# A hybrid decoder step in fp32: four dense projections by Strassen's scheme

## The chip, the core and the metric

The kernel runs on one core of a Trainium2 chip. The core has five engines that run their own instruction streams and meet at semaphores: TensorE (PE, matmuls from SBUF into PSUM), VectorE (DVE), ScalarE (ACT), GpSimd (POOL) and SyncE (SP, which issues the DMAs here). The metric is the device time of one execution in microseconds (us); smaller is better. All arithmetic here is fp32.

## The reference, cut to what matters

One layer step for 512 prompt tokens and 8 sample tokens, 520 in all: a sparse attention branch and a state-space branch, both from one normalised input, are mixed through gates and go through a gated feed-forward part. Only the end of it is changed:

```python
def merge_and_ffn(x, attn_o, ssm_o, ga, gm, w_attn_br, w_ssm_br, w_out, norm2_w, w_ffn_gate, w_ffn_up, w_ffn_down):
    mix = sigmoid(ga) * (attn_o @ w_attn_br) + sigmoid(gm) * (ssm_o @ w_ssm_br)
    x = x + mix @ w_out                                   # 1024 -> 1024, the out-projection
    h = rmsnorm(x, norm2_w)
    return x + (silu(h @ w_ffn_gate) * (h @ w_ffn_up)) @ w_ffn_down   # 1024 -> 2816 twice, 2816 -> 1024
# both outputs then go through rmsnorm(., normf_w)
```

## The kernel before, in words

**Layout.** Activations lie with features on the 128 partitions and the 520 tokens along the free axis: `xT` (the residual stream, 8 tiles of 128 features), `xn` (normalised, 8 tiles), `mix` (8 tiles), `hid` (22 tiles of the feed-forward's inner width), `stage` and `gate` (2 tiles each). Weights are streamed through `ring`, six slots of 1 MB, each holding 1024 rows (8 blocks of 128) by 256 columns of a weight matrix.

**A dense tile.** `dense` (the matmul is L351) makes one output tile of 128 features: for each of the row blocks k, two matmuls with the same 128x128 block of weights, one for each half of the tokens (TH = 260 columns), into a pair of PSUM banks. Two pairs of banks are used in turn. A tile of the out-projection, gate or up is 8 x 2 matmuls, one of down 22 x 2. So the part in question is 8 tiles of out-projection, 44 of gate and up, 8 of down.

**Around it.** ScalarE reads each finished tile out of PSUM (L1398 for out-projection and down, L1412, L1413 and L1417 in the feed-forward part), which frees the bank pair (`dense_read`). In `residual` VectorE adds the copy to `xT` (L1800), ScalarE squares the new tile (L421) and VectorE adds the squares up (L427); when all eight are in, TensorE sums over partitions (L379), ScalarE takes the root, VectorE the reciprocal, TensorE spreads it (L387, L388), ScalarE copies it (L405, L406), and VectorE writes the eight tiles of `xn` (L434). This happens after the out-projection (norm 2) and after down (final norm). In `ffn` ScalarE forms tanh of a half of the gate tile and a halved copy of it in `hid`, and VectorE multiplies (L1814) and then multiplies in the up tile (L1818).

**Order.** Each engine's order is its program text. TensorE: the attention part of the mix (4 steps of two gate tiles and two branch tiles), the out-projection, norm 2, gate and up in 11 steps of two gate and two up tiles, down, the final norm, the turning back of the output. SyncE loads the next block of weights into a slot as soon as `dense_done` says that the slot's tiles are done; four slots (5, 0, 1, 2) take gate and up in turn, 3 and 4 are filled early for down. GpSimd has nothing to do after the gathers of the decode part: its last work is L1929.

Of the kernel before, what the change touches and what calls it, by code (L numbers as in the profile page):

```python
# [76 lines left out]
def build(nc, x_prompt, x_sample, cache_k, cache_v, cache_idx_k, state_ssm, state_conv, page_table,  # L77
# [5 lines left out]
    with ExitStack() as ctx:  # L83
# [19 lines left out]
        gs = sb("gs", [32, GSEL])  # L103
# [188 lines left out]
        ytok, ystok = xtok, xstok  # L292
        raw_flat = raw.rearrange("p i t -> p (i t)")
# [10 lines left out]
        DOWN_SLOTS = [(3, 4, 1), (2, 5, 0)]  # L304
# [13 lines left out]
        F_DOWN = [21, 12, 16, 6, 6, 11]  # L318
# [10 lines left out]
        w_in_slot = [S(f"weights_in_slot{i}") for i in range(NSLOT)]  # L329
# [80 lines left out]
        def rms_pe(pe, i, e):  # L410
            pe.wait_ge(S("squares_added"), 7 * i + 5)
            sum_squares(pe, e, sqsum)
            spread_norm(pe, e)

        def square(act, i, k, ready=None):

            if ready is not None:
                act.wait_ge(S("res_added"), ready + k + 1)
            if k >= 3:
                act.wait_ge(S("squares_added"), 7 * i + k - 4)  # L420
            act.activation(sqsum if k == 0 else sq2[:, k % 2, :], xT[:, k, :], ACT.Square).then_inc(S("norm_squared"), 1)  # L421

        def add_square(v, i, k):
# [3 lines left out]
            v.tensor_tensor(sqsum, sqsum, sq2[:, k % 2, :], ALU.add).then_inc(S("squares_added"), 1)  # L427

        def rms_dve(v, i, e, w_col):
# [3 lines left out]
            for k in range(KT):  # L433
                v.scalar_tensor_tensor(xn[:, k, :], xT[:, k, :], vec[:, w_col + k:w_col + k + 1], rbc,  # L434
# [6 lines left out]
        def _(sp):  # L441
# [34 lines left out]
            sp.wait_ge(S("iqs_copied"), 1)  # L476
# [60 lines left out]
            def load_selectors(g):  # L537
                sp.dma_start(gs[:], gsel_d[bass.ds(g, 1)].rearrange("o p c -> (o p) c")
# [65 lines left out]
            for it in range(2):  # L604
                n = N_ATT + 14 if it == 0 else N_OUT + 2
                load(sp, FFN_SLOTS[it][0], w_block(w_ffn_gate, it * 256), n)
                load(sp, FFN_SLOTS[it][1], w_block(w_ffn_up, it * 256), n + 2)
            load(sp, 3, w_block(w_ffn_down, 0), N_OUT + 6)
            load(sp, 4, w_block(w_ffn_down, 0, k0=D), N_OUT + 8)
            with sp.Fori(0, 4) as k:  # L610
                for o in range(2):
                    load(sp, FFN_SLOTS[o][0], w_block(w_ffn_gate, 512 * k + 256 * (o + 2)), 8 * k + N_FFN + 4 * o + 2)
                    load(sp, FFN_SLOTS[o][1], w_block(w_ffn_up, 512 * k + 256 * (o + 2)), 8 * k + N_FFN + 4 * o + 4)
            load(sp, FFN_SLOTS[0][0], w_block(w_ffn_gate, 2560), N_FFN + 34)
            load(sp, FFN_SLOTS[0][1], w_block(w_ffn_up, 2560), N_FFN + 36)
            for it in range(4):
                for i, slot in enumerate(DOWN_SLOTS[it % 2]):
                    if it == 0 and i < 2:
                        continue
                    freed = N_DOWN + 2 * (it - 1) if it > 1 else {1: N_FFN + 38, 2: N_FFN + 40, 5: N_FFN + 42, 0: N_FFN + 44}[slot]  # L620
                    load(sp, slot, w_block(w_ffn_down, 256 * it, k0=D * i, kt=(8, 8, 6)[i]), freed)
# [14 lines left out]
        def _(pe):  # L636
# [103 lines left out]
            pe.wait_ge(S("ik_sq"), 1)  # L740
# [331 lines left out]
            def ffn(k, o):  # L1072
                for s in range(2):
                    slot = FFN_SLOTS[o][s]
                    pe.wait_ge(w_in_slot[slot], 16 * (k + F_FFN[slot] + 1))
                    for j in range(2):
                        first = isinstance(k, int) and k + o + s + j == 0
                        dense(pe, 8 * k + N_FFN + 4 * o + 2 * s + j, j, block_of(slot, j), xns,
                              ready=("norm_ready", KT) if first else None)

            ffn(0, 0)
            ffn(0, 1)
            with pe.Fori(1, 5) as k:
                ffn(k, 0)
                ffn(k, 1)
            ffn(5, 0)

            def down(it, k):

                slots = DOWN_SLOTS[it]  # L1090
                for s in slots:
                    pe.wait_ge(w_in_slot[s], 16 * (k + F_DOWN[s] + 1))
                for j in range(2):
                    blocks = block_of(slots[0], j) + block_of(slots[1], j) + block_of(slots[2], j, 6)
                    dense(pe, 4 * k + N_DOWN + 2 * it + j, j, blocks, [hid[:, i, :] for i in range(FT)],
                          ready=("hid_ready", 2 * OPEN) if isinstance(k, int) and k + it + j == 0 else None)

            down(0, 0)
            down(1, 0)
            down(0, 1)  # L1100
            down(1, 1)
            rms_pe(pe, 2, NORMF)

            pe.wait_ge(S("dense_read"), N_END)
# [13 lines left out]
        def _(act):  # L1118
# [21 lines left out]
            act.activation(taps, ps[:, 4, 128:256], ACT.Copy, scale=0.5).then_inc(S("taps_ready"), 1)  # L1140
            act.activation(dsk, ps[:, 4, 256:272], ACT.Copy).then_inc(S("dsk_ready"), 1)
# [7 lines left out]
            act.activation(hvec[0:32, 2:3], hvec[0:32, 1:2], ACT.Exp).then_inc(S("a_exp"), 1)  # L1149
            act.wait_ge(S("vector_mark"), IK_SQ_IN)  # L1150
            act.activation(ikt2, ikt1, ACT.Square).then_inc(S("ik_sq"), 1)
# [5 lines left out]
            act.activation(iqs, kviq[:, 4:12, SEQ:T], ACT.Copy).then_inc(S("iqs_copied"), 1)  # L1157
            act.wait_ge(S("tensor_mark"), IK_VAR)
            act.activation(two(ikt2), ps[:, 4:6, 0:TH], ACT.Sqrt, bias=eps[:, 0:1]).then_inc(S("ik_root"), 1)
# [5 lines left out]
            act.activation(actok, ps[:, 7, 256:384].rearrange("p (b h) -> p b h", h=32), ACT.Copy).then_inc(S("actok_ready"), 1)  # L1165
# [29 lines left out]
            act.activation(qkvs[:, 0:8, :], uT[:, :, SEQ:T], ACT.Copy).then_inc(S("qkvs_ready"), 1)  # L1195
            act.activation(qkvs[:, 8:12, :], kviq[:, 0:4, SEQ:T], ACT.Copy).then_inc(S("qkvs_ready"), 1)
# [192 lines left out]
            def residual(n0, before, i):  # L1389
                for n in range(8):  # L1390
                    act.wait_ge(S("dense_done"), n0 + n + 1)
                    if n >= 2:
                        act.wait_ge(S("res_added"), before + n - 1)
                    else:
                        act.wait_ge(S("mixed"), 16)
                        if before:
# [594 lines left out]
```

## Time and profile before

| | us |
|---|---|
| median of 3 runs | 1762.99 |
| lowest and highest | 1761.59, 1771.35 |
| the profiled execution's span (the page gives no other time of it) | 1790.0 |
| TensorE busy in the span | 1685.6 |
| VectorE, ScalarE, GpSimd busy | 764.1, 400.6, 217.7 |

A page is one execution, seen by the hardware profiler. "Busy" is the time in which an engine executes; "idle before" is the time in which it stood still just before an instruction, with what released it; the chain follows the last instruction back through whatever it waited for. One fp32 matmul leaves two records.

### The profile page before, as it was taken

To read this page: it belongs to the slowest core of one execution; us is meant where nothing else is said; L and a number is where in the kernel's file an instruction comes from. 1 tells how busy PE (TensorE), PEld (TensorE's weight loads), DVE (VectorE), ACT (ScalarE), POOL (GpSimd) and SP (SyncE) were. 2 spreads that over 40 slices of the span, in tenths; PEclk is the share of its full clock that TensorE was granted. 3 is DMA by queue.
4 is the path that set the end of the run, shared out by engine and by line. 5 is a ranking of instruction groups with operands and counts; after the bars stand their busy time and mean duration, and the time that the engine had idled before them with its cause. 6 is when DMAs were issued, how large, how long until landed. Compare 5 with 4: busy or idle time off the path is not lost. (4 is left out here: it accounts for less than half of the span.)

```text
span 1790.0 us, 21883 instructions
## 1 busy us (share of the span) xinstructions
PE 1685.6 (94%) x8411; PEld 1430.7 (80%) x8411; DVE 764.1 (43%) x1192; ACT 400.6 (22%) x855; POOL 217.7 (12%) x224
## 2 busy tenths in 40 slices
PE   6998998999999999999889799999999999999997
PEld 5886876887777778878768688888788888888886
DVE  3314886179989999898871000001120101000002
ACT  3013236224334342243320010000211111110002
POOL 1000110024122231241221500000000000000000
PEclk8998989999999999999999879899999999999997
DMA  6111122223313313221224404122212222221201
GB/s 196 47 36 48 47 66 79 72 68 83 95 54 97 97 54 96 56 72 47 78 71 139 123 1 141 48 71 83 82 48 71 83 81 70 70 65 56 92 0 48
DMA packets 153482, 131.12 MB, mean 73 GB/s; under 512 B 11410, under 2 KB 149938, under 8 KB 153410
## 3 DMA queue, kind: packets, MB, share of 16 engines
q1 hardware_dynamic: 150610, 121.93, 22.6%
q0 software_dynamic: 2816, 8.39, 1.6%
q8 instruction: 42, 0.69, 0.2%
q14 instruction: 14, 0.11, 0.0%
HBM read 117.26 MB, written 13.27 MB: 73 GB/s over the span
## 5 line engine op out<-in xcount | busy, mean ns | idle before, releaser
L351 PE MATMUL ps<-xn,ring 128*128 128x260 f32 x4160 | 945.4, 387 | 7.6 <-DVE xn L434 3.3
L351 PEld LDWEIGHTS ps<-xn,ring 128*128 128x128 f32 x4160 | 789.4, 191 | 134.2 <-issue 3.8
L351 PE MATMUL ps<-work,ring 128*128 128x260 f32 x960 | 210.7, 382 | 0.0
L351 PEld LDWEIGHTS ps<-work,ring 128*128 128x128 f32 x960 | 182.4, 190 | 28.0
L351 PE MATMUL ps<-ssm_o,ring 128*128 128x260 f32 x512 | 120.9, 399 | 2.8 <-issue 2.8
L351 PEld LDWEIGHTS ps<-ssm_o,ring 128*128 128x128 f32 x512 | 102.2, 200 | 20.4 <-issue 3.4
L1800 DVE TENSOR_TENSOR xT<-xT,work 128x520 f32<-128x520 f32 x16 | 11.2, 700 | 192.3 <-ACT work L1398 192.3
L1907 POOL TENSOR_TENSOR ring<-ring 128x512 f32<-128x512 f32 x32 | 40.5, 1265 | 331.8 <-ACT ring L1261 331.8
L1814 DVE SCALAR_TENSOR_TENSOR work<-work 128x520 f32 (+1 forms) x22 | 15.4, 700 | 145.9 <-ACT work L1413 145.9
L1596 DVE MAX8 work<-work 8x8 f32<-8x2049 f32 x32 | 72.8, 2273 | 0.6
L1601 DVE FIND_INDEX8 dix<-work 8x8 uint32<-8x2049 f32 x32 | 72.8, 2274 | 0.0
L1603 DVE MATCH_REPLACE8 work<-work 8x2049 f32<-8x2049 f32 x32 | 72.5, 2266 | 0.0
L1818 DVE TENSOR_TENSOR work<-work 128x520 f32 (+1 forms) x22 | 15.4, 700 | 130.8 <-ACT work L1417 130.8
L1635 DVE SCALAR_TENSOR_TENSOR work<-work 128x512 f32<-128x512 f32 x96 | 67.0, 769 | 7.3 <-ACT work L1271 7.3
L1734 DVE SCALAR_TENSOR_TENSOR work<-work 128x520 f32<-128x520 f32 x8 | 5.6, 700 | 136.7 <-ACT work L1351 114.5
L351 PE MATMUL ps<-uT,ring 128*128 128x260 f32 x256 | 59.6, 395 | 0.4 <-DVE uT L1784 0.4
L351 PEld LDWEIGHTS ps<-uT,ring 128*128 128x128 f32 x256 | 50.4, 198 | 8.7 <-DVE uT L1784 0.5
L1257 ACT ACTIVATE ring<-ps,work 128x128 f32<-128x128 f32 x128 | 36.5, 367 | 79.3 <-PE ps L910 79.3
L1398 ACT ACTIVATE work<-ps 128x520 f32<-128x520 f32 x16 | 9.7, 603 | 194.4 <-PE ps L351 194.4
L1231 ACT ACTIVATE work<-ps 128x520 f32<-128x520 f32 x32 | 18.2, 593 | 129.1 <-PE ps L351 129.1
L1790 DVE SCALAR_TENSOR_TENSOR work<-work 128x520 f32<-128x520 f32 x8 | 5.6, 700 | 91.8 <-ACT work L1387 91.8
L1417 ACT ACTIVATE work<-ps 128x520 f32<-128x520 f32 x22 | 13.3, 604 | 134.8 <-PE ps L351 134.8
(299 smaller groups left out, 1711.6 us busy)
## 6 DMA issues: line engine op xcount, KB each, us to landing
ring<-in_w_in SPq DMA_DIRECT2D x34, 1024.0 KB, 5.3
ring<-in_w_ffn_gate SPq DMA_DIRECT2D x11, 1024.0 KB, 5.3
ring<-in_w_ffn_up SPq DMA_DIRECT2D x11, 1024.0 KB, 5.3
ring<-in_w_in SPq DMA_DIRECT2D x16, 512.0 KB, 5.3
work<-in_state_ssm SPq DMA_DIRECT2D x16, 512.0 KB, 6.3
out<-work SPq DMA_DIRECT2D x16, 512.0 KB, 4.0
ring<-in_w_ssm_br SPq DMA_DIRECT2D x8, 1024.0 KB, 6.5
ring<-in_w_ffn_down SPq DMA_DIRECT2D x8, 1024.0 KB, 5.1
```

The lines of the kernel that those rows point to most:

```text
L351: mm = pe.matmul(ps[0:m, 2 * pair + h, 0:TH], lhs[k], rhs[k][:, h * TH:(h + 1) * TH], start=(k == 0), stop=(k == len(lhs) - 1))
L1231: act.activation(two(raw[:, i, 3:T + 3]), tile_out(i % 2), ACT.Copy).then_inc(S("dense_read"), 1)
L1257: act.activation(M2[:, c % 2, r * P:(r + 1) * P], abc[:, r * P:(r + 1) * P], ACT.Relu, scale=-1.0, bias=atg[:, c, r:r + 1]).then_inc(S("E_ ...
L1417: act.activation(two(stage[:, j, :]), tile_out(j), ACT.Copy).then_inc(S("dense_read"), 1)
L1596: v.max(best, row).then_inc(S("dtop_max"), 1)
L1601: v.max_index(dix[:], best, row).then_inc(S("dtop_index"), 1)
L1603: v.match_replace(row, best, row, -3.3e38).then_inc(S("dtop_cut"), 1)
L1635: v.scalar_tensor_tensor(xc[:, i, 0:SEQ], raw[:, i, t:t + SEQ], cw[:, 5 * i + t:5 * i + t + 1], xc[:, i, 0:SEQ], ALU.mult, ALU.add).then_i ...
L1800: v.tensor_tensor(xT[:, n, :], xT[:, n, :], stage[:, n % 2, :], ALU.add).then_inc(S("res_added"), 1)
L1814: v.scalar_tensor_tensor(hs[j], gate[:, j, :], 1.0, hs[j], ALU.add, ALU.mult).then_inc(S("silu_h"), 1)
L1818: v.tensor_tensor(hs[j], hs[j], stage[:, j, :], ALU.mult).then_inc(S("hid_ready"), 1)
L1907: g.tensor_tensor(m, m, CBm[:, c:c + 1, :].broadcast_to((P, 4, P)), ALU.mult).then_inc(S("M_ready"), 1)
```

## The change

Every pair of output tiles (256 columns of weights) of the out-projection, gate, up and down becomes one *unit*, numbered q: 0 to 3 out-projection, 4 to 25 gate and up in turn, 26 to 29 down. In a unit the weights are seen as 2 x 2 blocks, a11, a12, a21, a22 (first index the tile, second the parity of the row block), and the activations as b11, b12, b21, b22 (parity of the row block, half of the tokens). In place of eight block products there are seven, each a chain of 4 matmuls of 260 columns (11 in down):

- GpSimd makes, for each unit, s1 = a21 + a22, s3 = a11 - a21 (in place of a21), s2 = s1 - a11 and s4 = a12 - s2, each for all row pairs at once (128 x 512 elements, for down three pieces of 512, 512 and 384). It may start when the third product of the unit two before is done, since two sets of sum buffers are used in turn.
- VectorE makes, once for `mix`, `xn` and `hid`, the four sums of each pair of tiles: t1 = b12 - b11, t3 = b22 - b12, t2 = b22 - t1, t4 = b21 - t2 (260 columns each, t2 after t1, t4 after t2).
- TensorE's order within a unit is product 6 (s2 t2), 7 (s3 t3), 2 (a12 b21, added onto product 1 in its bank), 5 (s1 t1, onto product 6), then product 1 (a11 b11) of the next unit, then 3 (s4 b22, onto 6 and 5) and 4 (a22 t4, onto 7). Three banks are used by a unit, two sets in turn.
- ScalarE copies product 1 (`copy_1`) and the finished first quarter (`copy_11`); VectorE forms the other three quarters in five additions of 260 columns from PSUM (`add_u2`, `add_others`). What follows (residual, squares, tanh, multiplies) works on both tiles of a unit after that, instead of tile by tile.

The last three groups of down's weights go to space of `xn` and `uT` in turn with the ring; a slot is refilled after the last product of its unit (`load_after`) where it was after the tile before. Some semaphores of the first part are merged (`ik_sq`, `iqs_copied` and `ik_root` into `ik_steps`, `a_exp` into `dt_exp`, `taps_ready` and `dsk_ready` into `vec_ready`, `gone_ready` into `dpg_ready`), and `gs` gets 128 rows instead of 32, the rest used for sums.

The core of the diff:

```diff
+        def operands(q):
+            a = [[], [], [], [], [], [], []]
+            for (slot, n, _), (s1, s2, s4) in zip(units(q), pair_sums(q)):
+                parts = (quarter(slot, n, 0, 0), quarter(slot, n, 0, 1), s4, quarter(slot, n, 1, 1), s1, s2, quarter(slot, n, 1, 0))
+                for of, part in zip(a, parts):
+                    of += [part[:, k, :] for k in range(n)]
+            b, t = (MIX_B, MIX_T) if q < Q_FFN else (XN_B, XN_T) if q < Q_DOWN else (HID_B, HID_T)
+            return a, [b[0][0], b[1][0], b[1][1], t[3], t[0], t[1], t[2]]
...
+        def load_after(sp, q, slot, src):
+            sp.wait_ge(S("product_done"), 6 * q + DONE_4)
+            kt, n = src.shape[1], src.shape[2]
+            sp.dma_start(slots[slot][:, 0:kt, 0:n], src).then_inc(w_in_slot[slot], 16)
...
         @block.tensor
-            for u in range(4):
-                pe.wait_ge(w_in_slot[OUT_SLOTS[u]], 16 * (F_OUT[OUT_SLOTS[u]] + 1))
-                for j in range(2):
-                    dense(pe, N_OUT + 2 * u + j, j, block_of(OUT_SLOTS[u], j), [mix[:, k, :] for k in range(KT)],
-                          ready=("mixed", 8) if u + j == 0 else None)
+            def product_6(q, m0=0, m1=None, sums=None):
+                if m0 == 0:
+                    pe.wait_ge(S("weight_sums"), 4 * unit_number(q + 1) - 1)
+                    if q >= 2:
+                        pe.wait_ge(S("combined"), 5 * (q - 2) + MADE_C12)
+                mm = product(q, 1, 5, m0, m1, sums=None if sums is None else sums + 3)
+                if m1 is None:
+                    mm.then_inc(S("product_done"), 1)
+            def head(q, sums=None):
+                if q >= 2:
+                    pe.wait_ge(S("combined"), 5 * (q - 2) + MADE_C21)
+                product(q, 2, 6, sums=None if sums is None else sums + 2).then_inc(S("product_done"), 1)
+                pe.wait_ge(S("s1_copied"), q + 1)
+                product(q, 0, 1, start=False, stop=True).then_inc(S("product_done"), 1)
+                pe.wait_ge(S("combined"), 5 * q + MADE_U2)
+                product(q, 1, 4, start=False).then_inc(S("product_done"), 1)
+            def tail(q, sums=None):
+                pe.wait_ge(S("weight_sums"), 4 * unit_number(q + 1))
+                pe.wait_ge(S("combined"), 5 * q + MADE_U4)
+                product(q, 1, 2, start=False, stop=True).then_inc(S("product_done"), 1)
+                pe.wait_ge(S("combined"), 5 * q + MADE_C22)
+                product(q, 2, 3, start=False, stop=True, sums=None if sums is None else sums + 4).then_inc(S("product_done"), 1)
+            pe.wait_ge(S("dense_read"), N_OUT)
+            product_1(0, ready=("mixed", 8))
+            for q in range(Q_OUT, Q_FFN):
+                first = SUMS_MIX if q == Q_OUT else None
+                product_6(q, sums=first)
+                head(q, sums=first)
+                if q + 1 < Q_FFN:
+                    product_1(q + 1)
+                tail(q, sums=first)
             rms_pe(pe, 1, NORM2)
+            product_1(Q_FFN, ready=("norm_ready", KT))
...
         @block.scalar
+            def residual(q0, before, i):
+                for u in range(4):
...
+                        act.wait_ge(S("res_added"), before + 2 * u)
+                    copy_1(q0 + u, stages)
+                    if u:
+                        square(act, i, 2 * u - 2, before)
+                        square(act, i, 2 * u - 1, before)
+                    copy_11(q0 + u, stages)
...
         @block.vector
+            def sums(b, t, m, base):
+                v.tensor_tensor(t[0][m], b[0][1][m], b[0][0][m], ALU.subtract).then_inc(S("sums_made"), 1)
+                v.tensor_tensor(t[2][m], b[1][1][m], b[0][1][m], ALU.subtract).then_inc(S("sums_made"), 1)
+                v.wait_ge(S("sums_made"), base + 4 * m + 2)
+                v.tensor_tensor(t[1][m], b[1][1][m], t[0][m], ALU.subtract).then_inc(S("sums_made"), 1)
+                v.wait_ge(S("sums_made"), base + 4 * m + 3)
+                v.tensor_tensor(t[3][m], b[1][0][m], t[1][m], ALU.subtract).then_inc(S("sums_made"), 1)
...
             rms_dve(v, 1, NORM2, 8)
+            for m in range(4):
+                v.wait_ge(S("norm_ready"), KT + 2 * m + 2)
+                sums(XN_B, XN_T, m, SUMS_XN)
...
         @block.gpsimd
+            g.wait_ge(S("vector_mark"), DO_READY)
+            for q in range(Q_OUT, Q_END):
+                if q >= 2:
+                    g.wait_ge(S("product_done"), 6 * (q - 2) + DONE_3)
+                for i, ((slot, n, filled), (s1, s2, s4)) in enumerate(zip(units(q), pair_sums(q))):
...
+                    g.wait_ge(w_in_slot[slot], filled)
+                    g.tensor_tensor(s1, a21, a22, ALU.add).then_inc(S("weight_sums"), 1)
+                    g.wait_ge(S("weight_sums"), done + 1)
+                    g.tensor_tensor(a21, a11, a21, ALU.subtract).then_inc(S("weight_sums"), 1)
+                    g.tensor_tensor(s2, s1, a11, ALU.subtract).then_inc(S("weight_sums"), 1)
+                    g.wait_ge(S("weight_sums"), done + 3)
+                    g.tensor_tensor(s4, a12, s2, ALU.subtract).then_inc(S("weight_sums"), 1)
```

## Rows read from the trace of the kernel before

**Rows 1.** The page: engine totals, and the chain's shares by line.
```profile
PE 1685.6 (94%) x8411; PEld 1430.7 (80%) x8411; DVE 764.1 (43%) x1192; ACT 400.6 (22%) x855; POOL 217.7 (12%) x224
...
PE ps L351 42%; PE ps L1024 1%; PE ps L1056 1%; PE ps L387 0%; PE ps L1012 0%; PE ps L1112 0%; DVE xn L434 0%; PE ps L379 0%; PE ps L388 0%; ACT ssm_o L1431 0%; DVE ssm_o L427 0%; DVE xT L1800 0%; ACT ssm_o L421 0%; ACT work L1398 0%; ACT rt L395 0%
```

**Rows 2.** The chain from 1130 us: start, us, what, records.
```profile
1134.61 157.27 PE ps L351 x704
...
1291.91 0.61 ACT work L1398
...
1294.72 1.19 PE ps L379 x10
...
1300.44 464.86 PE ps L351 x2112
```

**Rows 3.** Timeline of TensorE: start, us, instruction, records, idle before.
```profile
1134.61 16.99 PE L351 MATMUL ps<-uT,ring 128*128 128x260 f32 x64 [0.43 <-DVE uT L1784]
1151.44 14.19 PE L351 MATMUL ps<-xn,ring 128*128 128x260 f32 x64
1165.47 14.19 PE L351 MATMUL ps<-uT,ring 128*128 128x260 f32 x64
...
1235.60 56.27 PE L351 MATMUL ps<-work,ring 128*128 128x260 f32 x256
```

**Rows 4.** Groups of instructions: count, busy us, mean ns, idle before.
```profile
L351 PE MATMUL ps<-work,ring 128*128 128x260 f32 x960 | 210.7, 382 | 0.0
```

**Rows 5.** The same view, GpSimd.
```profile
L1907 POOL TENSOR_TENSOR ring<-ring 128x512 f32<-128x512 f32 x32 | 40.5, 1265 | 331.8 <-ACT ring L1261 331.8
...
L1886 POOL TENSOR_TENSOR work<-work 128x32 f32<-128x32 f32 x24 | 13.6, 592 | 82.0 <-ACT work L1278 82.0
```

**Rows 6.** The page's DMA issues: count, KB each, us to landing.
```profile
ring<-in_w_ffn_gate SPq DMA_DIRECT2D x11, 1024.0 KB, 5.3
```

**Rows 7.** Timeline of VectorE, ops of 256 columns and what follows them.
```profile
430.70 0.42 DVE L1699 TENSOR_TENSOR work<-work 128x256 f32<-128x256 f32 x1 [0.71 <-PE ps L929]
431.16 0.42 DVE L1702 TENSOR_TENSOR work<-work,ps 128x256 f32<-128x256 f32 x1
431.50 0.74 DVE L1709 SCALAR_TENSOR_TENSOR work<-work,ps 128x512 f32<-128x512 f32 x1
```

**Rows 8.** Groups of instructions, ScalarE copying 256 columns from PSUM.
```profile
L1176 ACT ACTIVATE ssm_o<-ps 128x256 f32<-128x256 f32 x16 | 6.1, 382 | 12.5 <-DVE ssm_o L1509 11.3 <-PE ps L648 1.2
```

**Rows 9.** DMA issues from 1687 to 1730 us, three loads issued together.
```profile
ring<-in_w_ffn_down SPq DMA_DIRECT2D x1, 768.0 KB, 9.8
```

**Rows 10.** Timeline of GpSimd.
```profile
443.67 4.75 POOL L1901 TENSOR_TENSOR work<-work 128x1024 f32<-128x1024 f32 x2
```

**Rows 11.** Timeline of VectorE at the same time.
```profile
444.19 1.86 DVE L1639 TENSOR_TENSOR work<-work 128x16 f32<-128x16 f32 x1
445.98 3.61 DVE L1642 SCALAR_TENSOR_TENSOR work<-work 128x520 f32<-128x520 f32 x3
449.74 0.70 DVE L1642 SCALAR_TENSOR_TENSOR work<-work 128x520 f32<-128x520 f32 x1 [0.16 <-ACT work L1292]
```

**Rows 12.** Line L1639: ns at least, in the middle and at most.
```profile
L1639 DVE TENSOR_TENSOR work<-work x8: 221/1863/1867, 377.4 to 871.2; 128x16 f32<-128x16 f32 x8
```

**Rows 13.** Timeline of ScalarE at the end of the mix.
```profile
1235.80 0.60 ACT L1387 ACTIVATE work<-ps 128x520 f32<-128x520 f32 x1 [6.41 <-PE ps L351]
```

**Rows 14.** Timeline of VectorE there.
```profile
1237.17 0.70 DVE L1794 TENSOR_TENSOR work<-work 128x520 f32<-128x520 f32 x1
```

**Rows 15.** Timeline of VectorE at norm 2.
```profile
1299.54 5.46 DVE L434 SCALAR_TENSOR_TENSOR xn<-xT,vec,ssm_o 128x520 f32<-128x520 f32 x8 [2.96 <-ACT ssm_o L406]
```

**Rows 16.** Stretches there and behind: us, busy of PE, PEld, DVE, ACT, POOL, granted clock.
```profile
1301.00:1304.00 3.00, 3.00 (x8) 2.36 (x7) 3.00 (x5) 0.00 (x0) 0.00 (x0) 0.51 0.00 0
1304.00:1308.00 4.00, 4.00 (x20) 3.47 (x19) 0.99 (x2) 0.00 (x0) 0.00 (x0) 1.00 0.02 4
...
1320.00:1400.00 80.00, 80.00 (x366) 69.35 (x365) 7.70 (x11) 10.39 (x17) 0.00 (x0) 1.00 0.22 72
```

More of the change, by code:

```diff
@@ L331, in w_block, with banks @@
+        def banks(q):
+            return [3 * (q % 2) + i for i in range(3)]
         def w_block(w, c0, n=2 * P, k0=0, kt=KT):
@@ L1081, in _ @@
[L1081 to L1101, printed above, removed]
+            def product(q, bank, which, m0=0, m1=None, start=True, stop=False, sums=None):
+                a, b = operands(q)
+                lhs, rhs = a[which], b[which]
+                for m in range(m0, len(lhs) if m1 is None else m1):
+                    if sums is not None:
+                        pe.wait_ge(S("sums_made"), sums + 4 * m)
+                    mm = pe.matmul(ps[:, banks(q)[bank], 0:TH], lhs[m], rhs[m], start=start and m == 0,
+                                   stop=stop and m == len(lhs) - 1, skip_group_check=True)
+                return mm
@@ new lines, in _ @@
+            for q in range(Q_OUT, Q_FFN):
[5 more added lines that the diff above has]
+                tail(q, sums=first)
+            rms_pe(pe, 1, NORM2)
+            product_1(Q_FFN, ready=("norm_ready", KT))
+            for q in range(Q_FFN, Q_DOWN):
+                first = SUMS_XN if q == Q_FFN else None
+                product_6(q, sums=first)
+                head(q, sums=first)
+                if q + 1 < Q_DOWN:
+                    product_1(q + 1)
+                else:
+                    product_1(q + 1, m1=10, ready=("hid_ready", 0))
+                tail(q, sums=first)
@@ new lines, in _ @@
+            for q in range(Q_DOWN, Q_END):
+                first = SUMS_HID if q == Q_DOWN else None
+                if q == Q_DOWN:
+                    product_6(q, m1=10, sums=first)
+                    product_1(q, m0=10, ready=("hid_ready", 0))
+                    product_6(q, m0=10, sums=first)
+                else:
+                    product_6(q)
+                head(q, sums=first)
+                if q + 1 < Q_END:
+                    product_1(q + 1)
+                tail(q, sums=first)
@@ L1424, in _ @@
+            residual(Q_DOWN, KT, 2)
             root_norm(act, NORMF, D)
-            copy_norm(act, NORMF, rbc)
+            copy_norm(act, NORMF, rbcs[2])
             for b in range(5):
@@ new lines, in _ @@
+            for i in range(11):
+                q = Q_FFN + 2 * i
+                h = [hid[:, 2 * i, :], hid[:, 2 * i + 1, :]]
+                add_u2(q, h)
+                if i:
+                    hidden(i - 1)
+                add_others(q, h)
+                add_u2(q + 1, stages)
+                for j in range(2):
+                    v.wait_ge(S("gate_read"), 2 * i + j + 1)
+                    v.scalar_tensor_tensor(h[j], gate[:, j, :], 1.0, h[j], ALU.add, ALU.mult).then_inc(S("silu_h"), 1)
+                add_others(q + 1, stages)
@@ L1825, in _ @@
+            hidden(10)
+            residual(Q_DOWN, 2)
             rms_dve(v, 2, NORMF, 16)
```

294 lines of the change are left out of this document (191 added, 103 removed).

## The prediction

> **What bounds the kernel now.** I read the totals first: TensorE is busy for 1685.6 us of a span of 1790.0, and the chain of work that ended last is 42% line L351, the matmul of `dense` [rows 1]. The shares of the span are an average, so next I read that chain over the part that the change touches, from the last part of the mix to the end [rows 2]. It is one unbroken run of L351 from 1134.61 to 1291.88 us (the mix and the out-projection), a norm of 8.6 us in which TensorE has nearly nothing to do, and a second run from 1300.44 to 1765.30 (gate, up and down). Nothing else ends late there: VectorE and ScalarE only follow. The timeline of TensorE then gives the price of a matmul [rows 3]. 64 records start every 14.03 us, two records belong to one fp32 matmul (the out-projection has 8 tiles x 8 blocks x 2 halves = 128 matmuls and 256 records), so one matmul of 260 columns takes 14.03/32 = **0.4384 us**. The idle time of a group of 960 such records is 0.0, across all tile borders with their waits [rows 4]: a wait that is already satisfied shows no cost here.
>
> The sum is made against the profiled execution. Its span is 1790.0 us, 27.0 above the median of 1762.99, and the page gives no other time for it. All that is removed below lies where the granted clock is 1.00, as in the first 80 us of it [rows 16], so I take the microseconds off the median unscaled.
>
> **What it removes.** Out: 128 matmuls become 4 x 28 = 112. Gate and up: 704 become 22 x 28 = 616. Down: 352 become 4 x 77 = 308. That is 148 fewer, 148 x 0.4384 = **-64.9 us**, all on the path. The moving operand stays 260 columns wide and every matmul loaded its own weights before (one weight load per matmul record), so the price of one stays.
>
> **What it adds beside TensorE, in steady state.** Set time 0 where the sixth product of the unit before ends. A unit of 28 matmuls then takes 12.28 us, in blocks of 1.75: product 6, product 7, product 2 (needs ScalarE's copy of product 1), product 5 (needs the first VectorE sum), product 1 of the next unit, product 3, product 4 (each needs a VectorE read of its bank).
> GpSimd: 4 sums of 128x512 at 1.265 us [rows 5] are 5.1 us, and they may start at product 3 of the unit two before, so some 14 us are there for them. A load of 1 MB lands in 5.3 us [rows 6] with three units (37 us) to do it in. Both are hidden.
> VectorE: 256 columns take 0.42 us, from SBUF or with one operand in PSUM [rows 7]; ScalarE takes 0.38 to copy as many out of PSUM [rows 8]. The first sum waits for product 6 (1.75), is done at 2.2 and needed at 5.26. The one for bank 1 is done at 7.5 and needed at 8.77; bank 2 is read at 7.9 and needed at 10.52. In a gate or up unit the two multiplies (0.70 each) and the four sums of a pair of `hid` (1.6) fit between 2.2 and 7.0. So no handover is late, by margins of 1.2 us and more: cost 0. If that cover goes, the nearest row is TensorE's one wait on a short VectorE step, 0.43 us idle [rows 3]; one such in each of 30 units is +13 us. Between 0 and 13 I take 0, since the idle column reads 0.0 [rows 4], and keep 13 for the range.
> In the down units all these margins grow with the 11 pairs. The last of the three loads behind each lands in 9.8 us [rows 9]; their raw blocks are needed 44 matmuls (19.3 us) after the issue, their sums (12 of at most 1.265, 15.2 us) 33.8 us after it: hidden.
>
> **The lock between VectorE and GpSimd.** The rows show one [rows 10 to 12]. While two GpSimd sums ran from 443.67 to 448.42, a VectorE op on 128x16 with both operands in SBUF took 1.86 us (0.22 at its shortest) and the next op of 128x520 ended only with the second sum; right behind them the same op took 0.70. So a VectorE op with two SBUF operands sits out the GpSimd sum in progress, up to 1.27 us here. GpSimd's four sums run from -1.7 to about 3.4 in my unit's time, with VectorE's ops between them. In a gate or up unit this delays the multiplies to about 4.7 and the sums to 6.4, still before 7.0. In the out-projection it meets the residual adds, which free the staging tile for ScalarE's copy of product 1: the copy, ready at 2.3 without the lock, comes at about 3.8, 0.3 after product 2 wants it. Three units: **+0.9 us**.
> The Trainium skill says the same ("SBUF — State Buffer", section "Who interferes with whom"): a VectorE instruction with two SBUF inputs and a GpSimd instruction that reads SBUF exclude one another, and whoever comes second is blocked. The trace agrees, 1.86 us against 0.22; without that rule and row the two lock terms of my sum would be nothing and the forecast about 1707.
>
> **What it adds on the path.**
> Start of the out-projection: before, its first tile only waited for the tile before the last to be read. Now it waits for ScalarE's last copy, 1235.80 + 0.60 [rows 13]. TensorE idles from 1235.6 to about 1236.4: **+0.75**. The last pair sum that product 6 needs is ready at 1237.87 + 0.34 + 0.45 + 0.42 = 1239.1 [rows 7, 14], wanted at 1239.5: no cost.
> Tail before the norm: before, the last matmul was followed by a copy, an add, a square and an add, until 1294.72: 2.83 us [rows 2]. Now both tiles of the pair end together: a sum of 260 columns, two adds, two squares and two adds, pipelined 3.2 us, so +0.4 for each of two norms. At the first norm GpSimd's sums for the first up unit run at the same time (their buffers came free at product 3 of the last out unit). By the lock, the second add ends at 3.4 instead of 1.7 and the last square's add at 6.0 instead of 3.2: +2.8. Together **+3.6** (bounds 0.8 without the lock, 5.9 with four full waits of 1.27).
> First gate unit: this is the largest term. Before, TensorE followed VectorE's eight `xn` tiles one by one, starting 0.9 us after the first. Now product 1 needs every second tile, and product 6 needs sums that VectorE makes only after all eight, 5.46 us from 1299.54 [rows 15]. A pair's four sums depend on each other; by starts of 0.34 (independent) and 0.46, taken as 0.45 (dependent) [rows 7] a pair takes 1.58 us, and the third sum of the fourth pair is there at 1305.0 + 3 x 1.58 + 0.34 + 0.45 + 0.42 = 1310.95. TensorE has done 8 matmuls by 1311.8 (the last at half clock). The other 916 take 401.6. The granted clock was 0.51 from 1301 to 1304 and 1.00 after it [rows 16]: TensorE had run its first 3.5 us behind the pause at the lower of its two levels (1.2 of 2.4 GHz), which costs 1.75. I expect the same behind the new pause. The end is then 1715.1 against 1765.30, a gain of 50.2 where 132 matmuls fewer would give 57.9: **+7.7**. Bounds: 5.9 if the clock has come back by then, 9.5 if it stays low as long again.
> Semaphores merged under one name in the first 1130 us keep their order and their engines: 0, and 1 us either way for what I miss.
>
> **Sum:** -64.9 + 0.9 + 0.75 + 3.6 + 7.7 = -51.95. 1762.99 - 51.95 = **1711.0 us**.
>
> **The rivals.**
> *Handovers are not free.* The unit splits 28 matmuls into seven chains with some ten waits, where a tile had 16 behind one or two. For it: margins of 1.2 us rest on ops that no row shows with these very operands. Against it: 0.0 idle in 960 records [rows 4]. At 0.43 a unit: 1711.0 + 13 = 1724.
> *VectorE late in each unit.* If the lock lets GpSimd's sums through in a row, an op waits for two of them. In the out, gate and up units a delay of 2 x 1.27 against a margin of 1.26 at bank 1 stalls 1.28 us x 22 units or so: 1711 + 28 = 1739. Against it: GpSimd's sums are over by about 4.7 and the bank 1 sum has only one SBUF operand, while the lock's rows are of two.
> *GpSimd becomes the bound, slower than before.* A unit took 32 x 0.4384 = 14.03 us before; GpSimd decides from 14.03/4 = 3.5 us a sum. For it: GpSimd's strided op on 128x32 took 592 ns [rows 5], 18.5 ns a column, and the new sums read blocks out of a wider tile; at half of that rate a sum of 512 takes 4.7 us. A unit would be 18.9 us, 26 units +127, four down units (56.9 against 38.6) +73: about 1960; at 3.75 us a sum it is still 1815. Against it: the runs here are 128 columns long, as in L1907, which took 1265.
> *The saving isn't there* (the count of matmul records does not fall, or each gets dearer): the same, near 1763. Against it: price and count above.
>
> **Chances.** Forecast 0.68, its own range 1703 to 1718 (the bounds of tail, first gate unit and spread of runs). Handovers 0.20, late VectorE 0.06, no saving 0.02, GpSimd 0.04. The runs before spread over 1761.6 to 1771.4, so 0.5% is about what a measurement tells from no change. Faster: 0.68 + 0.20 + 0.06 = 0.94; same 0.02; slower 0.04. The low end is 1703, all lower bounds together; at the high end 1731 takes in the handovers with the upper bound of the lock.
>
> **What would show it.** Right: 2072 records of L351's successors for out, gate, up and down instead of 2368, still 0.219 us apart; some 12 us from the first `xn` tile to the first dense stretch; VectorE's residual adds over 1 us where a GpSimd sum runs; the stretch from there to the last matmul near 403 us. Wrong: idle of TensorE spread over all units with VectorE or ScalarE as releaser (handovers), with GpSimd as releaser (GpSimd bound), or a record that takes longer than before.

## The result and the profile after

The changed kernel takes **1717.44 us** (median of 4 runs, 1712.1 to 1719.38) against 1763.23 before (median of 4 as well): ratio 0.9717 with a 95% interval of 0.9685 to 0.975, faster. The forecast was 1711.0 with a range of 1703 to 1731. A second set of runs, made for the experiments, gave 1719.23 and 0.9726 [0.9698, 0.9753].

The page of after, and the chain from the end of the mix (start, us, what, records), answer to [rows 1, 2]:

```profile
PE 1616.8 (94%) x8115; PEld 1363.1 (80%) x8115; DVE 884.9 (52%) x1418; ACT 385.9 (23%) x851; POOL 420.1 (25%) x376
...
PE ps L1166 22%; PE ps L445 14%; PE ps L1182 4%; PE ps L1149 1%; DVE xT L2000 1%; DVE xn L528 1%; PE ps L1117 0%; PE ps L481 0%; PE ps L1260 0%; PE ps L473 0%; PE ps L1105 0%; DVE ssm_o L521 0%; DVE uT L1953 0%; ACT ssm_o L1592 0%; DVE work L521 0%
```

```profile
1210.26 0.61 ACT work L1535
...
1250.98 2.81 DVE xT L2000 x2
1253.81 0.40 ACT work L1540
...
1258.06 0.44 DVE work L1977
...
1265.56 1.69 DVE ssm_o L521
...
1274.15 5.46 DVE xn L528 x8
...
1285.14 0.44 DVE uT L1953
1285.63 7.04 PE ps L1166 x26
...
1294.43 10.52 PE ps L1166 x48
...
1306.70 10.52 PE ps L1166 x48
```

L1166 and L1182 are the matmul of a product (L1182 is product 1). TensorE has 8115 records where it had 8411: 296 fewer, two for each of 148 matmuls. What was one run of L351 is now cut at a few places: ScalarE's last copy of the mix (L1535), VectorE's residual adds (L2000), which hold back the copy of product 1 (L1540), its first read of a bank in the last unit (L1977), the sums before the norm (L521), `xn` and the pair sums. From 1285.63 on the chain is TensorE alone as far as the end of down's last unit but one, and a unit of gate or up returns every 12.27 us (1294.43, 1306.70).

**Where the time went, by stage.** Each stage is measured on the timeline of one profiled execution, from the end of the mix's last matmul on. "Front edits" is the experiment e_front, which computes as before did and whose profiled run took 1763.59 us, near its median of 1764.57.

| us | before | front edits | after |
|---|---|---|---|
| end of the mix | 1235.6 | 1207.1 | 1210.1 |
| to the last matmul of the out-projection | 56.27 | 56.27 | 52.32 |
| to norm 2's first sum on TensorE | 2.85 | 2.84 | 5.72 |
| to the first tile of `xn` | 4.82 | 5.25 | 6.05 |
| to the last matmul of down | 465.75 | 466.84 | 415.63 |
| final norm and the rest | 24.71 | 23.51 | 24.02 |
| **from the mix to the end** | **554.4** | **554.7** | **503.7** |

The changed part took 50.7 to 51.0 us less, where the forecast said 51.95. The medians differ by 45.8 only: the runs of either kernel fall into two groups (means 1763.1 and 1771.1 before, 1713.7 and 1719.4 after), group against group the gain is 49.4 and 51.7, but the middle run of before lies in the shorter group and that of after in the longer. The difference arises in the first part, where TensorE does the same work in both kernels. After's profiled execution reached the end of the mix at 1210.1 us and a second one at 1213.5, where four variants of it with the same first part (e_defer, e_xn, e_best, e_pool2) reached it at 1205.1 to 1207.7.

The first 1200 us also clear up the profiled execution of before: it reached the end of the mix 28.5 us later than e_front did with the same instructions, which is the excess that the prediction left out by taking its sum off the median.

### The profile page after: what moved, and what is told of

Read it like the earlier page. It is cut to its first block and busy times, and to the rows that moved or that the text cites. A ratio compares the mean times of both kernels' runs of the same rounds, so it can differ in the third digit from the quotient of the medians.

```text
span 1713.8 us, 21557 instructions
## 1 busy us (share of the span) xinstructions
PE 1616.8 (94%) x8115; PEld 1363.1 (80%) x8115; DVE 884.9 (52%) x1418; ACT 385.9 (23%) x851; POOL 420.1 (25%) x376
## 5 line engine op out<-in xcount | busy, mean ns | idle before, releaser
L445 PE MATMUL ps<-xn,ring 128*128 128x260 f32 (+1 forms) x2752 | 639.0, 390 | 6.0 <-ACT work L1303 1.9
L445 PEld LDWEIGHTS ps<-xn,ring 128*128 128x128 f32 (+1 forms) x2752 | 523.7, 193 | 92.4 <-ACT work L1303 2.3
L445 PE MATMUL ps<-ssm_o,ring 128*128 128x260 f32 x512 | 114.6, 386 | 0.0
L445 PEld LDWEIGHTS ps<-ssm_o,ring 128*128 128x128 f32 x512 | 98.2, 192 | 15.3
L2158 POOL TENSOR_TENSOR work<-ring 128x512 f32<-128x512 f32 (+1 forms) x15 | 18.5, 1233 | 276.4 <-PE ps L1166 154.1
L1166 PE MATMUL ps<-uT,ring 128*128 128x260 f32 x352 | 84.9, 384 | 0.0
L1166 PEld LDWEIGHTS ps<-uT,ring 128*128 128x128 f32 x352 | 67.5, 192 | 10.6
L1977 DVE TENSOR_TENSOR work<-ps,work 128x260 f32<-128x260 f32 x30 | 12.9, 429 | 101.8 <-PE ps L1166 101.8
L1981 DVE TENSOR_TENSOR work<-ps,work 128x260 f32<-128x260 f32 x30 | 12.9, 429 | 100.8 <-PE ps L1166 100.8
L445 PE MATMUL ps<-uT,ring 128*128 128x260 f32 x256 | 58.8, 392 | 0.4 <-DVE uT L1944 0.4
L445 PEld LDWEIGHTS ps<-uT,ring 128*128 128x128 f32 x256 | 49.9, 196 | 8.5 <-DVE uT L1944 0.5
L1545 ACT ACTIVATE work<-ps 128x260 f32<-128x260 f32 x30 | 11.6, 387 | 191.4 <-PE ps L1166 191.4
L1540 ACT ACTIVATE work<-ps 128x260 f32<-128x260 f32 x30 | 11.6, 388 | 179.8 <-DVE xT L2000 91.2
L2057 POOL DMA_INDIRECT work<-in_cache_idx_k,gidx x16 | 15.7, 980 | 134.0 <-DVE gidx L1639 73.2
```

The costliest lines, as they stand in the source:

```text
L445: mm = pe.matmul(ps[0:m, 2 * pair + h, 0:TH], lhs[k], rhs[k][:, h * TH:(h + 1) * TH], start=(k == 0), stop=(k == len(lhs) - 1))
L1166: mm = pe.matmul(ps[:, banks(q)[bank], 0:TH], lhs[m], rhs[m], start=start and m == 0, stop=stop and m == len(lhs) - 1, skip_group_check=True)
L2158: g.tensor_tensor(s1, a21, a22, ALU.add).then_inc(S("weight_sums"), 1)
```

## The experiments

**The same kernel again,** beside e_defer, e_xn and e_best on one chip (e_front, e_eight and e_pool2 ran on another, each set with runs of the kernel before):

> The changed kernel once more, unaltered, as the measure for the variants beside it. My theory: TensorE's saving of 64.9 us less about 14 us on the path, so 49 to 52 us below the kernel before. Rival: the first 1210 us got some us slower too (merged semaphores), so 44 to 47 us below it.

1719.23 us (1713.4 to 1720.58, 5 runs). By the medians that is 44.7 us below before (1763.97 in this set), the rival's figure and not the theory's; the rival's reason, the merged semaphores, is ruled out by the next experiment, and by stages the theory holds: from the mix to the end 503.9 us, each stage within 0.3 of the table. So the whole of that part repeats within 0.3 us, as it does for before and e_front (554.4 and 554.7). A single stage is less sure: before and e_front, with the same instructions there, differ by 1.1 us up to the last matmul of down and by 1.2 in the rest.

**Do the edits of the first part cost anything?** The kernel before, with the merged semaphores and the larger `gs` and nothing else:

```diff
-        gs = sb("gs", [32, GSEL])
+        gs_all = sb("gs", [P, GSEL])
+        gs = gs_all[0:32]
...
-            v.wait_ge(S("ik_root"), 1)
+            v.wait_ge(S("ik_steps"), 3)
```

> The kernel before with only the changes of the first 1130 us: merged semaphores, gs with 128 rows; all matmuls as before. My theory: no difference, within 1 us of the kernel before. Rival: the 3 to 5 us that the median gives less than the two traces' last part lie here, so 3 us or more slower than the kernel before.

1764.57 us against 1764.69, ratio 1.0001 [0.9983, 1.0018]: nothing, to within 3 us.

**Is the saving the price of the matmuls?** Product 7 is run twice in each unit (its result is the same), so TensorE has the 148 matmuls back and everything else stays:

```diff
-                product(q, 2, 6, sums=None if sums is None else sums + 2).then_inc(S("product_done"), 1)
+                product(q, 2, 6, sums=None if sums is None else sums + 2)
+                product(q, 2, 6).then_inc(S("product_done"), 1)
```

> The changed kernel with product 7 of each unit run twice into the same bank, so eight block products again (148 more fp32 matmuls; the result is the same). Theory: a matmul costs 0.4384 us and nothing else is late, so 64.9 us above the changed kernel, less about 1.2 because the repeated product hides the late copy in the out-projection: 62 to 65 us more, some 13 to 19 us slower than the kernel before. Rival (units are paced by handovers, not by TensorE): clearly less than 60 us more.

1780.68 us (1773.13 to 1785.61), ratio 1.0078 [1.0047, 1.0108] to before, 16.0 us slower than it as the theory had it. From the mix to the end 568.2 us, 64.4 more than after. That is 148 x 0.4384 = 64.9, less the 1.2 that the copy of product 1 no longer costs in the out-projection, and 0.7 more in the first gate unit, where the granted clock rose later in this execution. TensorE's timeline in it, one product 1 to the next:

```profile
1331.48 1.92 PE L1182 MATMUL ps<-xn,ring 128*128 128x260 f32 x8
...
1345.51 1.92 PE L1182 MATMUL ps<-xn,ring 128*128 128x260 f32 x8
```

The unit is 14.03 us, as 32 matmuls were before [rows 3], and 1.75 more than after's 12.27, the price of four. This kernel multiplies as often as before and makes all of the scheme's additions, and is 13.5 us longer behind the mix than e_front (568.2 - 554.7): the price of the scheme's new order, against which the saving stands (13.9 in after itself, 64.9 - 51.0).

**The lock, taken away where it was forecast to hurt.** GpSimd's sums for units 2 to 4 wait for the residual adds of the unit two before, where in after they start at the end of product 3 of that unit (the last but one of its products to run), just ahead of the adds. Those of unit 5 wait for the pair sums of `xn`. So the two engines don't overlap there:

```diff
+                if 2 <= q <= 4:
+                    g.wait_ge(S("res_added"), 2 * (q - 1))
+                if q == 5:
+                    g.wait_ge(S("sums_made"), SUMS_HID)
```

> GpSimd's weight sums for units 2 to 4 start only behind the residual adds of the unit two before, those for unit 5 behind VectorE's sums of xn. Lock theory: out-projection units 12.28 us apart instead of 12.69 (1.2 us), the tail before norm 2 about 3.2 us instead of 5.75 (2.5 us), the norm itself up to 1.2 us shorter because the pause before it is shorter; together 3.7 to 5 us faster than the changed kernel. Rival (the ops are late for their own lengths or their semaphores, not for GpSimd): under 1 us, and the adds stay at 1.06 us each.

1712.6 us (1704.41 to 1717.86), ratio 0.9695 [0.9664, 0.9726]. The out-projection took 51.07 instead of 52.32, the sums before norm 2 3.33 instead of 5.72: -3.6 in all, as the lock theory had it for those two places. The norm itself did not get shorter, which the theory had allowed up to 1.2 us for. (The interval overlaps with after's, here and in e_xn below, so the stages are the surer figure.) The residual adds by line (ns at least, in the middle, at most), first in after:

```profile
L2000 DVE TENSOR_TENSOR xT<-xT,work x16: 687/904/1760, 1225.6 to 1690.8; 128x520 f32<-128x520 f32 x16
```

and in e_defer:

```profile
L2000 DVE TENSOR_TENSOR xT<-xT,work x16: 689/692/695, 1223.2 to 1684.8; 128x520 f32<-128x520 f32 x16
```

All 16 adds fall to 0.69 us once GpSimd is still. TensorE's timeline agrees: product 2 in two units in a row, 12.28 us apart, where after's are 12.69 apart (1228.87, 1241.56, 1254.25):

```profile
1213.88 1.92 PE L1166 MATMUL ps<-work,ring 128*128 128x260 f32 x8
...
1226.16 1.92 PE L1166 MATMUL ps<-work,ring 128*128 128x260 f32 x8
```

**The lock, doubled.** For the units before down GpSimd makes its sums over again (s1 three times, s2 and s4 twice, s3, which is made in place, once), each operation waiting for the one before: 8 operations for 4. It decides between a GpSimd that is merely busier (hidden still, since 8 x 1.27 = 10.2 us is under a unit's 12.28) and one that slows VectorE:

```diff
...
+                    for _ in range(3 if q < Q_DOWN else 1):
+                        steps(g.tensor_tensor(s1, a21, a22, ALU.add))
...
+                    for _ in range(twice):
+                        steps(g.tensor_tensor(s4, a12, s2, ALU.subtract))
```

> GpSimd does each weight sum of the out, gate and up units twice (the first kind three times, the in-place one once: eight ops of 1.27 us in place of four), each waiting for the one before. Lock theory with turns: a VectorE op with two SBUF operands waits out one sum, so in a gate unit two multiplies and four sums of hid end near 13 us instead of 5.4, VectorE's read of product 5's bank comes some 4 us late, in ten gate units: 30 to 50 us slower than the changed kernel. Rival 1 (no lock that matters, GpSimd 10.8 us of 12.3 still fits): within 3 us. Rival 2 (GpSimd becomes the bound because its sums wait for VectorE too): units of 14 us and more throughout, 45 us or more slower, TensorE released by GpSimd rather than VectorE.

1742.65 us (1740.83 to 1751.14), ratio 0.9885 [0.9857, 0.9913] to before; from the mix to the end 533.8, 29.9 more than after: the low end of the forecast (30 to 50; by the medians 23.4). TensorE's waits in it (us, times, longest):

```profile
PE ps L1166 <- DVE work L1977: 20.7, 12, 2.0
PE ps L473 <- DVE ssm_o L521: 6.9, 1, 6.9
```

VectorE, GpSimd and TensorE around one of the ten late units of gate and up, each from its own timeline:

```profile
1363.24 2.38 DVE L2017 SCALAR_TENSOR_TENSOR work<-work 128x520 f32<-128x520 f32 x2
1365.65 1.38 DVE L1950 TENSOR_TENSOR ssm_o<-work 128x260 f32<-128x260 f32 x1
...
1369.89 1.37 DVE L1955 TENSOR_TENSOR ssm_o<-work,ssm_o 128x260 f32<-128x260 f32 x1
1371.19 0.41 DVE L1977 TENSOR_TENSOR work<-ps,work 128x260 f32<-128x260 f32 x1
```

```profile
1355.89 2.61 POOL L2166 TENSOR_TENSOR work<-ring,work 128x512 f32<-128x512 f32 x2
...
1363.45 1.61 POOL L2162 TENSOR_TENSOR ring<-ring 128x512 f32<-128x512 f32 x1
1365.14 3.03 POOL L2164 TENSOR_TENSOR xdt<-xdt,ring 128x512 f32<-128x512 f32 x2
1368.24 2.74 POOL L2166 TENSOR_TENSOR gs<-ring,xdt 128x512 f32<-128x512 f32 x2
```

```profile
1371.75 1.99 PE L1166 MATMUL ps<-xn,work 128*128 128x260 f32 x8 [1.96 <-DVE work L1977]
```

Here the rival "VectorE late in each unit" has come true by force, in every second unit of gate and up. Its six operations with two SBUF operands take 8.0 us where alone they take some 3, so the read of bank 1 (L1977) comes late by up to 2 us (the theory had some 4), in 10 of 22 units (in the others no sums of `hid` are due). GpSimd is not itself the bound: product 3 here reads the sums in `work`, which were done at 1358.50; those that end at 1370.98, in `gs`, are for the next unit. The wait before norm 2 grew as well, from 5.7 to 6.9 us.

The stalls explain less than the whole. Each makes its unit 2.2 us longer, 21.8 in all. In three of the ten (at 1398.49, 1480.38 and 1562.29) the granted clock fell behind the stall to its lower level, and the unit took 16.15 us where the other stalled ones took 14.46: another 5.1. A stretch behind the first of the three (us, busy of PE, PEld, DVE, ACT, POOL, granted clock):

```profile
1400.00:1402.00 2.00, 2.00 (x6) 1.51 (x5) 0.00 (x0) 0.00 (x0) 0.00 (x0) 0.50 0.00 0
```

Behind the other seven stalls, as long, it stayed at 1.00; why it fell behind three stays open.

**The first gate unit, in another order.** VectorE makes the first two sums of all four pairs, then all third, then all fourth; TensorE runs product 2, which needs none of the sums, between products 1 and 6:

```diff
...
+                    product(q, 0, 1, start=False, stop=True)
...
+                    product(q, 1, 5, sums=[SUMS_XN + n for n in (3, 5, 7, 8)]).then_inc(S("product_done"), 1)
...
+                    product(q, 2, 6, sums=[SUMS_XN + 9 + m for m in range(4)]).then_inc(S("product_done"), 2)
```

> Only the first gate unit is reordered: VectorE makes the sums that product 6 needs for all four pairs first, then those of product 7, then those of product 4, and TensorE runs product 2 (which needs none) between product 1 and product 6. Theory (TensorE waits for VectorE's chain there): the twelfth matmul of the unit ends about 11.5 us after the first xn tile instead of 14.9, so 3 to 4 us faster than the changed kernel, some 0.5 more or less by when the granted clock returns to 1.00. Rival (the stall is set by the clock or by the weights' sums): under 1 us.

1709.96 us (1705.77 to 1716.8), ratio 0.9689 [0.9662, 0.9717]; from the first `xn` to the last matmul of down 412.7 us instead of 415.6: -2.9, just under the 3 to 4 of the theory. TensorE behind norm 2, first in after:

```profile
1275.06 5.17 PE L1182 MATMUL ps<-xn,ring 128*128 128x260 f32 x8 [1.64 <-DVE xn L528]
1280.90 1.21 PE L1166 MATMUL ps<-uT,work 128*128 128x260 f32 x2 [0.67 <-DVE uT L1953]
...
1286.66 2.51 PE L1166 MATMUL ps<-uT,ring 128*128 128x260 f32 x8
1289.00 1.92 PE L1166 MATMUL ps<-xn,ring 128*128 128x260 f32 x8
...
1292.51 1.92 PE L1182 MATMUL ps<-xn,ring 128*128 128x260 f32 x8
```

and in e_xn:

```profile
1270.24 5.17 PE L1182 MATMUL ps<-xn,ring 128*128 128x260 f32 x8 [1.64 <-DVE xn L528]
1275.97 3.69 PE L1166 MATMUL ps<-xn,ring 128*128 128x260 f32 x8 [0.57 <-ACT work L1553]
...
1284.76 1.92 PE L1182 MATMUL ps<-xn,ring 128*128 128x260 f32 x8
```

Where after ran product 6 two records at a time, each pair behind VectorE, all chains have their 8 records in one, and the next unit's product 1 starts 15.43 us after the first `xn` (1269.33) instead of 18.36 (1274.15). In either order this time varies with the moment at which the granted clock rises: 18.36 to 19.26 in after, after_again, e_defer and e_pool2, 15.43 here and 16.19 in e_best.

**Both together, and the last units.** The last units of the out-projection and of down have no product 1 of a next unit between product 5 and product 3, so VectorE's read of the bank stands open: two waits of 0.61 us in after. Here products 5 and 2 change places in these two units (with what waits for them):

```diff
...
+                if q in LAST:
+                    pe.wait_ge(S("combined"), 5 * q + MADE_U2)
+                    product(q, 1, 4, start=False).then_inc(S("product_done"), 1)
...
```

> Both of these together, and in the last unit of the out-projection and of down products 5 and 2 change places, so that VectorE's read of product 5's bank lies under product 2 (TensorE waits 0.6 us there in each, with no product 1 of a next unit in between). The three are on the path one after another and should add up: 3.7 to 5, 3 to 4, and 1.2, so 8 to 10 us faster than the changed kernel, about 1708. Rival: one of the waits hides behind another and under 6 us come.

**1708.8 us** (1705.25 to 1713.13), ratio 0.9677 [0.9652, 0.9702], the shortest median of the kernels here; from the mix to the end 496.0 us, 7.8 less than after, just under the forecast of 8 to 10. It is 3.6 and 2.9 as above, 0.85 from each swap, 0.3 in the norm, and 0.8 lost again in the first gate unit. Both waits on L1977 are gone. In the out-projection the swap shows as 50.22 against 51.07 in e_defer. In down it shows from product 1 of the second gate unit on (1283.14; 1284.76 in e_xn): 396.4 us to the last matmul against 397.3. Measured from the first `xn` only 0.1 of it is left, since the granted clock rose later in this execution: TensorE's products 2 and 6 behind norm 2 took 6.03 us together, 5.28 in e_xn. The two intervals of after's and e_best's ratios to before overlap slightly (0.9698 against 0.9702), so of the 10 us between their medians the 7.8 that the stages show are the surer figure.

## Why the prediction was right

The terms of its sum, each with what stands for it in after (against e_front, stage by stage):

| term | forecast | measured | from |
|---|---|---|---|
| 148 matmuls | -64.9 | -64.9 | e_eight's units against after's, 1.75 for each four |
| start of the out-projection | +0.75 | +1.0 | e_best's 50.22 less 112 matmuls at the old pace (56.27 - 16 x 0.4384) |
| copy late in three units, the lock | +0.9 | +1.2 | e_defer, 52.32 - 51.07 |
| last unit of out, of down | 0 | +1.7 | 0.85 each by the swap in e_best |
| sums before the two norms | +3.6 | +3.4 | 2.88 and 0.50 in the table's stages |
| norm 2 itself | 0 | +0.8 | 6.05 - 5.25 |
| first gate unit | +7.7 | +5.8 | 415.63 - (466.84 - 132 x 0.4384), less the 0.85 of down |

The measured column adds up to -51.0, as the stages do. The mechanism held term by term; that the sum came within 1 us is in part luck, since 3.0 us that were charged too low or not at all (start, copy, last units, norm) stand against 2.1 that were charged too high (first gate unit, sums).

*The saving.* Price and count held. The steady state cost nothing: TensorE's waits from the out-projection to the final norm (us, times, longest) are few, and none lies in units 5 to 28:

```profile
PE ps L473 <- DVE ssm_o L521: 5.7, 1, 5.7
PE ps L473 <- DVE work L521: 3.3, 1, 3.3
PE ps L1166 <- DVE uT L1953: 1.7, 4, 0.7
...
PE ps L1166 <- DVE work L1977: 1.2, 2, 0.6
```

With that the first rival ("handovers are not free", 1724) falls, and with it the two whose mark would have been idle time in all units; the fourth ("the saving isn't there") falls by the count of records and the 12.27 us of a unit. The second was a fair rival: in e_pool2 twice the work on GpSimd was enough for it.

*The lock.* It was read from one place of the trace, where two other lines ran side by side [rows 10 to 12], and it came about where it was forecast. VectorE at the sums before norm 2, then GpSimd at the same time (after, two timelines):

```profile
1262.77 2.79 DVE L2000 TENSOR_TENSOR xT<-xT,work 128x520 f32<-128x520 f32 x2
1265.48 2.56 DVE L521 TENSOR_TENSOR ssm_o<-ssm_o 128x520 f32<-128x520 f32 x2
```

```profile
1263.28 1.72 POOL L2161 TENSOR_TENSOR xdt<-xdt,ring 128x512 f32<-128x512 f32 x1
1265.08 1.60 POOL L2163 TENSOR_TENSOR gs<-ring,xdt 128x512 f32<-128x512 f32 x1
```

The add that the prediction let end 3.4 us after the last matmul ended at 1265.56, 3.2 after it (1262.38). Groups of VectorE's lines behind the mix (count, busy us, mean ns, idle before) show which operations the lock reaches:

```profile
L2032 DVE SCALAR_TENSOR_TENSOR work<-work 128x520 f32<-128x520 f32 x22 | 26.1, 1227 | 0.0
L2000 DVE TENSOR_TENSOR xT<-xT,work 128x520 f32<-128x520 f32 x16 | 16.4, 1064 | 0.0
...
L1983 DVE TENSOR_TENSOR work<-ps,work 128x260 f32<-128x260 f32 x30 | 12.9, 429 | 52.0 <-PE ps L1166 52.0
```

A multiply with both operands in SBUF takes 1.23 us where 0.70 is its time alone [rows 11], and an addition with one operand in PSUM takes 0.43 (0.42 for 256 columns in [rows 7]): 25 of the 30 of L1983 run for the most part beside a GpSimd sum, and all 30 take 427 to 430 ns. The Trainium skill ("SBUF — State Buffer", section "Who interferes with whom") draws the line at the same place: a VectorE instruction with two SBUF inputs contends with a GpSimd instruction that reads SBUF, one with at most one such input, outside VectorE's two-port modes, doesn't. The trace agrees, 1.23 against 0.70 us and 0.43 either way; that the delay costs time on the path is what e_defer shows.

*The first gate unit.* The third sum of the fourth pair was forecast 11.41 us after the first `xn`; it was there after 11.42 (L1953 from 1285.14, 0.43). The clock did what was forecast in kind, but not for as long (us, busy of PE, PEld, DVE, ACT, POOL, granted clock):

```profile
1285.00:1288.00 3.00, 2.63 (x7) 1.93 (x7) 1.40 (x4) 0.00 (x0) 0.00 (x0) 0.53 0.00 0
1288.00:1292.00 4.00, 4.00 (x20) 3.48 (x19) 0.00 (x0) 0.39 (x1) 0.00 (x0) 1.00 0.00 0
```

Behind product 6 the prediction gave 1.75 us to the lower level; product 7 there took 2.34 us (1286.66 to 1289.00) instead of 1.75, so 0.6 was lost. The same code lost 1.5 in e_pool2 (3.25 us, 1283.11 to 1286.36): the size of this loss differs from execution to execution. The size of the term, 5.8 against 7.7, also depends on what it is compared with: against the profiled execution of before, on which the forecast rests, it is 415.63 - (465.75 - 57.87) = 7.75, less the 0.85 of down 6.9. That execution had 1.1 us less in this stage than e_front.

*What was not foreseen* costs 2.5 us. The seven products keep VectorE's read off the path by putting product 1 of the next unit behind product 5; the last unit of a run has no next one, and the prediction's margin (7.5 ready, 8.77 wanted) had counted it in. And norm 2 was longer by 0.8 us: the granted clock is at its lower level (0.50) when its sums run, where e_front had 0.80 for as long a stretch, partly still at the upper one. The clock windows at these sums, after and then e_front:

```profile
1268.00:1271.00 3.00, 2.17 (x11) 2.06 (x12) 0.26 (x3) 0.40 (x2) 0.00 (x0) 0.50 0.01 3
```

```profile
1266.00:1269.00 3.00, 2.06 (x14) 1.95 (x15) 0.36 (x3) 1.10 (x3) 0.00 (x0) 0.80 0.62 213
```

The sums take 1.99 us in after, 1.18 in e_front. The longer pause ahead of them (5.7 against 2.8 us) suggests itself, but in e_defer it is 3.3 and they still take 1.99, in e_best it is 3.3 and they take 1.71, and at the final norm of before they take 2.00 behind a pause of 2.85: the pause alone doesn't decide, and what does stays open.

Of the 6.4 us between 1711.0 and the measured 1717.44, the changed part holds about 1. The rest lies in the first 1210 us, which the prediction took to be the same in both medians; that the median still fell within 1718, the upper end of the forecast's own range, owes nothing to the mechanism.

## What to carry to other kernels

Where one engine is the only one on the chain, work can be moved off it at its full price (148 matmuls, 64.9 us), as long as each handover's margin is worked out op by op; what is lost is lost at the ends of runs, where the next unit that hides a wait is missing. Before giving idle GpSimd a share, look for VectorE operations with both operands in SBUF that sit on a path of their own (here before a norm), and hold GpSimd back just there: two waits gave back 3.6 us. And take a difference of a few us from the stages that changed, not only from the medians, when the unchanged part of a kernel varies by as much; mind that even the stages of two executions of the same instructions differed by up to 1.2 us here.

## What the runs showed of the hardware

- *The lock works both ways and turn by turn.* In e_pool2, with GpSimd nearly always at work, VectorE's two-operand sums of 260 columns took 1.37 to 1.49 us each (0.43 alone), and GpSimd's sums of 512 were lengthened as well, to 1.61 in e_pool2 and 1.72 in after against 1.27. In the lines of e_pool2 above, VectorE's sums end at 1368.45 and 1371.26, each 0.28 us behind one of GpSimd's (1368.17 and 1370.98), which reads as one operation of either engine at a time.
- *A stall of 2 us can cost nearly twice as much.* In e_pool2 the granted clock fell to 0.50 behind three of ten such stalls of TensorE, and each of the three cost 1.7 us more.
- *The same stretch of small matmuls takes 10.9 or 15.3 us, by the granted clock.* Between two long stretches of dense matmuls TensorE turns keys with matmuls of 128 and of 4 columns. In after's execution of 1713.8 us (L1105 and L1117, TensorE's timeline):

```profile
1015.82 1.09 PE L1105 MATMUL ps<-cst,work 128*128 128x128 f32 x8
...
1019.83 0.95 PE L1117 MATMUL ps<-work 128*128 128x4 f32 x8
...
1026.72 14.27 PE L445 MATMUL ps<-ssm_o,ring 128*128 128x260 f32 x64
```

and in the same kernel's execution of 1717.4 us:

```profile
1012.70 1.09 PE L1105 MATMUL ps<-cst,work 128*128 128x128 f32 x8
...
1019.85 1.71 PE L1117 MATMUL ps<-work 128*128 128x4 f32 x8
...
1028.03 16.37 PE L445 MATMUL ps<-ssm_o,ring 128*128 128x260 f32 x64
```

From about 1018 us on, the second runs each group of 8 in 1.71 us instead of 0.95 and takes 2.1 us more for the first 64 dense records: 6.5 us together. What differs is the granted clock, 1.00 in the first (1016 to 1026 us) and this in the second:

```profile
1018.00:1028.00 10.00, 10.00 (x54) 10.00 (x53) 0.00 (x0) 2.39 (x4) 1.54 (x2) 0.53 0.16 42
```

It fell although TensorE did not stop: it was busy for 5.75 of the 6 us before, at 1.00, and for all of these 10. (The first execution had come to this stretch 3.1 us later, so the two spans differ by 3.6 only.) e_eight's profile shows the same, with 0.54; those of e_front, e_defer, e_xn, e_best and e_pool2 don't. Why the clock falls in one execution and not in another was not tried and stays open.
